# A recurrence's small products merged into fewer groups, with one place in PSUM per chunk

## The chip, the cores and the metric

The kernel runs on one core of one Trainium2 chip. The metric is the device time of one execution in microseconds, lower is better. The core has TensorE (matmul; its weight loads are a row of their own in the profile), VectorE, ScalarE, GpSimd (POOL) and SyncE (SP), each with a queue of its own that runs in program order, and DMA queues. Engines wait for each other by semaphores. Matmul results go to PSUM, in banks of 512 fp32 columns, and are read from there by VectorE or ScalarE.

## The reference, cut to what matters

One transformer block: a gated feed-forward part, a mixer, a cross attention to a memory, and a second feed-forward part. The mixer has two halves, side by side: eight heads of sparse attention and eight heads of a recurrence (RWKV-7). The change touches only the recurrence:

```python
def step(state, inp):
    r_t, w_t, k_t, v_t, kk_t, a_t = inp
    sa = jnp.einsum('bhvk,bhk->bhv', state, -kk_t)
    state = (state * w_t[:, :, None, :] + sa[..., None] * (kk_t * a_t)[:, :, None, :]
             + v_t[..., None] * k_t[:, :, None, :])
    return state, jnp.einsum('bhvk,bhk->bhv', state, r_t)
...
mu = jnp.mean(y, -1, keepdims=True)
var = jnp.mean(jnp.square(y - mu), -1, keepdims=True)
y = ((y - mu) * lax.rsqrt(var + RWKV_GN_EPS)).reshape(B, T, C)
```

## The kernel before

The sequence has 1,024 positions, and the recurrence is computed in 16 chunks of 64 (`NCH`, `CH`), each chunk for all eight heads, held as four pairs of 64 + 64 partitions (`PAIRS`). All its products are 64 rows by 64: those of a pair's first head use one corner of TensorE's array (rows and columns 0 to 63), those of the second the opposite one, so two run at a time. Eight products (four pairs by two heads) make one group; groups that write 128 columns are called wide.

Within a chunk, `gram_b`, `gram_k` and `gram_l` multiply the chunk's operands AR, B and K with each other; VectorE masks the results into GB, GK and L. `turn_a`, `turn_b` and `turn_k` turn (transpose) A, B and K by a product with the unit matrix `eye`. `x` multiplies GK by V. Then a triangular matrix is inverted by doubling, in five levels: `y0` to `y4` multiply the level's mask of GB (LTm, made by GpSimd) with T0; ScalarE copies the result to Y1; `t` and `tt` multiply it with the factor TT0, and VectorE adds the results to T0 and to TT0. T0 and TT0 are one matrix and its transpose, both carried along. `start` (lines 2081 and 2083) makes the first TT0 on VectorE. `wu`, `gr`, `s` and `out` make the state's step and the output, `mean` and `var` the normalisation: the mean comes from a product with `mean_pair`, VectorE subtracts it, ScalarE squares, a second product sums, VectorE inverts (`inverse`, line 2087).

Two chunks are under way at once. Each has its own tiles (`j` is the chunk's number modulo 2) and two banks of PSUM (`ps[j]`, used as `bank(j, 0)` and `bank(j, 1)`), and consecutive groups alternate between them.

The same stage, `attend_and_recur`, also does the attention half, on the same engines. One score step is `score` (TensorE, to `ar_s_ps`), `max` (VectorE: mask and smallest negative value, line 1999), `exp` (ScalarE) and `scale` (VectorE). `bank` transposes probabilities on TensorE, `copy` takes them to SBUF, `values` multiplies them by V, `finish` takes the result. The attention keeps one place for scores, so a score step waits for the `max` of the one before.

The order of all this is set by `joint_plan`. It is a list scheduler that runs when the program is built: every operation is an event with an engine, an assumed duration and the events that it needs, `in_order` replays them and picks on each engine the ready one of the longest remaining chain. It adds 0.1 us when TensorE's tiling changes (whole array, halves of columns for `values`, corners for the recurrence) and prefers to stay in one. Every engine then issues its events in that fixed order, whatever the real durations are. The masks and tables are loaded at the stage's start from ScalarE's queue, the values, keys and the next chunks' operands from SyncE's.

## Time and profile before

| what | value |
|---|---|
| time, median of 3 runs | 2672.34 us (2670.58 to 2675.16) |
| profiled execution, its own time | 2671.66 us |
| its span, first to last instruction | 2669.8 us |
| TensorE busy, share of the span | 97% |
| VectorE, ScalarE, GpSimd | 66%, 39%, 3% |
| the stage with the recurrence | 1083 to about 1665 us |

The span is that of one profiled execution; what lies around it (1.9 us) is launch and end. Busy time is the time in which at least one instruction of an engine runs; matmuls overlap each other, and their ends are modelled, so short stops of TensorE can hide in it. In a timeline row the first number is the start, the second the length; "idle before" is how long the engine stood, and the name behind the arrow is what it waited for. An fp32 product stands in the records twice, so a group of eight has 16 records. A name such as `ar_TT` is the tile TT0 of either chunk.

### The profile page before, as it was taken

Reading aid. Unit: us, or ns where it says so; the run is one execution under the profiler, and the core shown is the slowest. Engines: PE = TensorE matmul, PEld = TensorE weight load, DVE = VectorE, ACT = ScalarE, POOL = GpSimd, SP = SyncE. Lnnn points to the kernel's source line nnn. Section 1 sums busy time; section 2 is a strip of 40 time slices with the busy share of each in tenths; the row PEclk is TensorE's granted clock in tenths of the full one; section 3 lists DMA queues with packets and bytes.
Section 4 is the critical chain, followed back from the end, with each engine's and each line's share of the span. In section 5 each row is a group of like instructions: output and inputs, shape, how many; then the busy total and the mean of one; then the engine's idle time right before and its main releaser. Section 6 shows DMA issues by size and latency. Waiting matters only on the chain. (4 is left out here: it accounts for less than half of the span.)

```text
span 2669.8 us, 46706 instructions
## 1 busy us (share of the span) xinstructions
PE 2600.5 (97%) x19152; PEld 2151.7 (81%) x19152; DVE 1765.2 (66%) x2819; ACT 1041.2 (39%) x1839; POOL 88.0 (3%) x121
## 2 busy tenths in 40 slices
PE   8999999999999999899999998999999999999998
PEld 7788888888777788888888887777778788888887
DVE  6877667678344564577777775853446867667676
ACT  4332223445433534344444444542343332223443
POOL 0000000000000000111111110000000000000000
PEclk9999999999999999899999999999999999999999
DMA  4332335454423388521111110630022332335454
GB/s 143 111 105 76 118 114 180 151 196 155 99 95 102 104 265 219 138 50 36 34 38 38 30 42 6 248 135 1 32 102 80 110 116 70 113 114 192 139 190 145
DMA packets 268722, 295.65 MB, mean 111 GB/s; under 512 B 64898, under 2 KB 199296, under 8 KB 268544
## 3 DMA queue, kind: packets, MB, share of 16 engines
q1 hardware_dynamic: 265808, 290.47, 34.2%
q10 hardware_dynamic: 2736, 2.65, 0.4%
q8 instruction: 131, 2.15, 0.3%
q14 instruction: 47, 0.39, 0.0%
HBM read 206.47 MB, written 81.36 MB: 108 GB/s over the span
## 5 line engine op out<-in xcount | busy, mean ns | idle before, releaser
L1141 PE MATMUL f_ps<-hi,f_wh 128*128 128x512 f32 x672 | 263.1, 391 | 4.1 <-DVE f_wl L847 4.1
L1143 PE MATMUL f_ps<-hi,f_wl 128*128 128x512 f32 x672 | 262.9, 391 | 0.0
L2543 PE MATMUL f_ps<-hi,f_ahead_h 128*128 128x512 f32 x392 | 164.0, 418 | 0.8 <-PEq L72 0.8
L2544 PE MATMUL f_ps<-one_lo,f_ahead_h 128*128 128x512 f32 x392 | 153.6, 392 | 0.0
L2545 PE MATMUL f_ps<-hi,f_ahead_l 128*128 128x512 f32 x392 | 153.6, 392 | 0.0
L1141 PE MATMUL f_ps<-f_t3h,f_t2h 128*128 128x512 f32 x392 | 152.5, 389 | 0.0
L1142 PE MATMUL f_ps<-f_t3l,f_t2h 128*128 128x512 f32 x392 | 152.5, 389 | 0.0
L1143 PE MATMUL f_ps<-f_t3h,f_t2l 128*128 128x512 f32 x392 | 152.5, 389 | 0.0
L1141 PEld LDWEIGHTS f_ps<-hi,f_wh 128*128 128x128 f32 x672 | 127.0, 189 | 31.2 <-DVE f_wl L847 4.9
L1143 PEld LDWEIGHTS f_ps<-hi,f_wl 128*128 128x128 f32 x672 | 126.7, 189 | 26.4
L1142 PE MATMUL f_ps<-one_lo,f_wh 128*128 128x512 f32 x352 | 137.6, 391 | 0.0
L905 DVE TENSOR_TENSOR one_y<-f_ps,one_y 128x1024 f32<-128x1024 f32 x60 | 72.6, 1222 | 90.2 <-PE f_ps L1143 90.2
L905 DVE TENSOR_TENSOR y<-f_ps,y 128x1024 f32<-128x1024 f32 x60 | 72.6, 1222 | 90.2 <-PE f_ps L1143 90.2
L1142 PE MATMUL f_ps<-two_lo,f_wh 128*128 128x512 f32 x320 | 125.1, 391 | 0.0
L3270 PE MATMUL mt_d_ps<-mt_wh,hi 128*128 128x512 f32 x224 | 94.7, 423 | 10.1 <-DVE two_lo L3493 10.1
L2543 PEld LDWEIGHTS f_ps<-hi,f_ahead_h 128*128 128x128 f32 x392 | 74.0, 189 | 24.7 <-issue 10.4
L2544 PEld LDWEIGHTS f_ps<-one_lo,f_ahead_h 128*128 128x128 f32 x392 | 74.1, 189 | 18.5 <-issue 4.1
L3270 PE MATMUL mt_d_ps<-mt_wh,two_lo 128*128 128x512 f32 x224 | 88.2, 394 | 0.0
L3270 PE MATMUL mt_d_ps<-mt_wl,hi 128*128 128x512 f32 x224 | 88.2, 394 | 0.0
L2545 PEld LDWEIGHTS f_ps<-hi,f_ahead_l 128*128 128x128 f32 x392 | 74.0, 189 | 15.9
L1141 PEld LDWEIGHTS f_ps<-f_t3h,f_t2h 128*128 128x128 f32 x392 | 73.6, 188 | 15.4
L1143 PEld LDWEIGHTS f_ps<-f_t3h,f_t2l 128*128 128x128 f32 x392 | 73.6, 188 | 15.3
(584 smaller groups left out, 6830.4 us busy)
## 6 DMA issues: line engine op xcount, KB each, us to landing
act<-one_y SPq DMA_DIRECT2D x30, 512.0 KB, 3.5
f_work<-act SPq DMA_DIRECT2D x30, 512.0 KB, 3.6
act<-y SPq DMA_DIRECT2D x30, 512.0 KB, 3.6
arena<-act SPq DMA_DIRECT2D x30, 512.0 KB, 3.7
one_y<-in_w_in SPq DMA_DIRECT2D x25, 512.0 KB, 4.4
early<-in_ffn_w_gate SPq DMA_DIRECT2D x11, 1024.0 KB, 6.2
early<-in_ffn_w_up SPq DMA_DIRECT2D x11, 1024.0 KB, 8.7
f_raw<-in_ffn_w_gate SPq DMA_DIRECT2D x10, 1024.0 KB, 6.2
```

The costliest lines, as they stand in the source:

```text
L905: nc.vector.tensor_tensor(out, a, b, op).then_inc(joined, 1)
L1141: nc.tensor.matmul(out, wh, xh, start=start, stop=False)
L1142: nc.tensor.matmul(out, wh, xl, start=False, stop=False)
L1143: return nc.tensor.matmul(out, wl, xh, start=False, stop=stop)
L2543: nc.tensor.matmul(dense_ps[:, b, cols], w_hi[:, b, k, :], hi[:, k, cols], start=(k == 0), stop=False)
L2544: nc.tensor.matmul(dense_ps[:, b, cols], w_hi[:, b, k, :], lo[:, k, cols], start=False, stop=False)
L2545: mm = nc.tensor.matmul(dense_ps[:, b, cols], w_lo[:, b, k, :], hi[:, k, cols], start=False, stop=(k == KD - 1))
L3270: mm = nc.tensor.matmul(bank(n, b), lhsT[:, k, at], rhs[:, k, to], start=(k == 0 and x_ == 0), stop=(k == KD - 1 and x_ == 2))
```

## The change

It concerns the recurrence in `attend_and_recur`, its plan and one table. The operations, group by group:

- `gram_l` becomes a second part of `gram_b`: 16 products, one signal. VectorE reads it with two operations, GB and L, in a row.
- `turn_b` and `turn_k` become one group `turn_bk` of 16, `turn_a` and `x` one group `ax` of 16. ScalarE reads each with one copy of 512 columns for two of 256.
- In each level, `y` and a turning of T0 (a product with `eye`) are one group `yt` of 16, read by one copy of 512 columns into YT. The products `tt` and their adds on VectorE are gone for levels 0 to 3; in the last level `tf` makes the one result that is needed. `start` is gone.
- The mean is subtracted on TensorE, by a product with the table `center` (unit matrix less the mean). ScalarE copies the result to yT and squares it straight from PSUM.
- Each chunk has one place in PSUM, over both its banks: pairs 0 and 1 in the first, 2 and 3 in the second. Each group therefore waits until the group before it in its chunk has been read. `out` now waits for the reading of `s`.
- SyncE loads the next operands behind `ax` and no longer behind `turn_k`. `center` is one more load at the end of the tables.
- The plan has new assumed durations and needs; GpSimd's masking is due after `gram_b` rather than after `start`.

```diff
 FIRST_FILL = [FILLS.index((u, 0)) for u in range(UNITS)] + [len(FILLS)]
-PRODUCTS = ["gram_b", "gram_k", "gram_l", "turn_a", "turn_b", "turn_k", "x",
-            *[f"{w}{lv}" for lv in range(LEVELS) for w in (("y", "t", "tt") if lv + 1 < LEVELS else ("y", "tt"))],
-            "wu", "gr", "s", "out", "mean", "var"]
-TO_DVE = {"gram_b", "gram_k", "gram_l", "gr", "s", "mean", *[f"{w}{lv}" for lv in range(LEVELS) for w in ("t", "tt")]}
+PRODUCTS = ["gram_b", "gram_k", "turn_bk", "ax", *[f"{w}{lv}" for lv in range(LEVELS) for w in ("yt", "t") if (w, lv) != ("t", LEVELS - 1)],
+            "tf", "wu", "gr", "s", "out", "mean", "var"]
+TO_DVE = {"gram_b", "gram_k", "gr", "s", "tf", *[f"t{lv}" for lv in range(LEVELS - 1)]}
...
             before = {"gram_b": [out_of("var", c - 2)],
...
+                      "yt0": [out_of("ax"), ("masked", c)],
                       "s": [out_of("gr"), out_of("s", c - 1)],
-                      "out": [("rw", c, "s")],
-                      "mean": [out_of("out"), out_of("s")],
-                      "var": [("square", c)]}.get(name, [out_of(last)])
...
+                      "var": [("square", c)]}.get(name, [n and out_of(PRODUCTS[n - 1])])
...
-            if name == "gram_l":
-                event(("start", c), "dve", 0.6, out_of(name))
-                event(("masked", c), "pool", 4.6, ("start", c))
+            if name == "gram_b":
+                event(("masked", c), "pool", 4.6, out_of(name))
...
-        GB, GK, L = two("GB", 3, CH), two("GK", 2, CH), two("L", CH)
-        Ktok, AX = two("Kt", CH), two("AX", 2, CH)
+        GB, GK, L, AX = two("GB", 4, CH), two("GK", 2, CH), two("L", CH), two("AX", 2, CH)
...
-        T0, TT0, Y1 = two("T0", CH), two("TT0", CH), two("Y1", CH)
+        T0, YT = two("T0", CH), two("YT", 2, CH)
...
-                def at(k, p, h, width=CH):
-                    return ps[j][rows(h), k, p * width:(p + 1) * width]
+                def at(p, r, block, width=CH):
+                    return ps[j][rows(r), p // 2, (p % 2 * 4 + block) * CH:(p % 2 * 4 + block) * CH + width]
+
+                corners = [(p, r) for p in range(PAIRS) for r in range(2)]
+
+                def group(*parts):
+
+                    for block, lhsT_of, rhs_of, width in parts:
+                        for p, r in corners:
+                            mm = nc.tensor.matmul(at(p, r, block, width), lhsT_of(p)[rows(r)], rhs_of(p)[rows(r)], start=True, stop=True)
                     mm.then_inc(products[j], 1)
...
-                    group(0, B[j], AR[j], 2 * CH)
+                    group((0, lambda p: B[j][:, p], lambda p: flat(AR[j][:, p]), 2 * CH),
+                          (2, lambda p: AR[j][:, p][:, 0, :], lambda p: B[j][:, p], CH))
...
                     dve("gram_k")
+                    group((0, lambda p: B[j][:, p], unit, CH), (1, lambda p: K[j][:, p], unit, CH))
+                elif name == "ax":
+                    act("turn_bk")
                     pe.wait_ge(V_in[j], 32 * (c // 2 + 1))
-                    group(0, GK[j][:, :, 0, :], V[j])
...
+                    group((0, lambda p: AR[j][:, p, 0, :], unit, CH), (1, lambda p: GK[j][:, p, 0, :], lambda p: V[j][:, p], CH))
...
-                    group(0, LTm[j][:, lv], T0[j])
-                elif name[:2] == "tt":
-                    act(f"y{name[2:]}")
-                    group(0, Y1[j], TT0[j])
+                    group((0, lambda p: LTm[j][:, lv, p], lambda p: T0[j][:, p], CH), (1, lambda p: T0[j][:, p], unit, CH))
+                elif name == "tf":
+                    act(f"yt{LEVELS - 1}")
+                    group((0, lambda p: YT[j][:, p, 0, :], lambda p: YT[j][:, p, 1, :], CH))
                 elif name[0] == "t":
-                    act(f"y{name[1:]}")
-                    group(1, TT0[j], Y1[j])
+                    act(f"yt{name[1:]}")
+                    group((0, lambda p: YT[j][:, p, 1, :], lambda p: YT[j][:, p, 0, :], CH))
...
                 elif name == "out":
...
+                    pe.wait_ge(state, c + 1)
...
-                elif name[0] == "y":
-                    copy(Y1[j][:], bank(j, 0))
+                elif name[:2] == "yt":
+                    copy(both(YT[j][:]), result(j, 0, 2 * CH))
...
+                elif name == "mean":
+                    copy(yT[:, :, chunk(c)], features(j).rearrange("p (q c) -> p q c", c=CH))
...
-                    act.wait_ge(by_dve[j], through(dn, c, "mean"))
-                    nc.scalar.activation(ysq[j][:], yT[:, :, chunk(c)], ACT.Square).then_inc(by_act[j], 1)
+                    act.wait_ge(products[j], through(pn, c, "mean"))
+                    nc.scalar.activation(ysq[j][:].rearrange("p q c -> p (q c)"), features(j), ACT.Square).then_inc(by_act[j], 1)
...
+                    op(both(GB[j][:, :, 0:2, :]), result(j, 0, 2 * CH), gram_mask, ALU.mult)
+                    op(by_bank(L[j][:]), result(j, 2), all_pairs(m_low[:]), ALU.mult)
...
-                elif name[:2] == "tt":
-                    op(TT0[j][:], bank(j, 0), TT0[j][:], ALU.add)
+                elif name == "tf":
+                    op(by_bank(YT[j][:, :, 1, :]), result(j, 0), by_bank(YT[j][:, :, 1, :]), ALU.add)
...
-                    dve.wait_ge(by_act[j], through(an, c, "out"))
-                    op(yT[:, :, chunk(c)], yb[j][:], bank(j, 1), ALU.subtract)
...
-                elif e[0] == "start":
...
-                    nc.vector.tensor_tensor(TT0[j][:], GB[j][:, :, 0, :], over_pairs(m_one[:, 1]), ALU.mult).then_inc(by_dve[j], 1)
-                    dve.wait_ge(by_dve[j], through(dn, c, "one_t"))
-                    nc.vector.tensor_tensor(TT0[j][:], TT0[j][:], over_pairs(eye[:]), ALU.add).then_inc(by_dve[j], 1)
...
+        "center": np.eye(P, dtype=f) - same.astype(f) / f(CH),
```

Since the plan is computed anew, the events of attention stand elsewhere between those of the recurrence too. On TensorE, at the stage's opening, before (`ar_ps0` and `ar_ps1` are the places of chunk 0 and 1, `ar_s_ps` a score product):

```order
L1798 MATMUL ar_ps0<-chunk_ops 64x64 x8
L1798 MATMUL ar_ps1<-chunk_ops 64x64 x8
L1804 MATMUL ar_ps0<-ar_eye,chunk_ops 64x64 x8
L1804 MATMUL ar_ps1<-ar_eye,chunk_ops 64x64 x8
L1804 MATMUL ar_ps0<-ar_eye,chunk_ops 64x64 x8
L1804 MATMUL ar_ps1<-ar_eye,chunk_ops 64x64 x8
L1804 MATMUL ar_ps0<-ar_eye,chunk_ops 64x64 x8
L1804 MATMUL ar_ps1<-ar_eye,chunk_ops 64x64 x8
L1798 MATMUL ar_ps0<-ar_V0,ar_GK0 64x64 x8
L1798 MATMUL ar_ps1<-ar_V1,ar_GK1 64x64 x8
L1736 MATMUL ar_s_ps<-hi 128x128
L1737 MATMUL ar_s_ps<-hi 128x128
```

and now:

```order
L1797 MATMUL ar_ps0<-chunk_ops 64x128 x8
L1797 MATMUL ar_ps0<-chunk_ops 64x64 x8
L1797 MATMUL ar_ps1<-chunk_ops 64x128 x8
L1797 MATMUL ar_ps1<-chunk_ops 64x64 x8
L1735 MATMUL ar_s_ps<-hi 128x128
L1736 MATMUL ar_s_ps<-hi 128x128
L1797 MATMUL ar_ps0<-chunk_ops 64x128 x8
L1797 MATMUL ar_ps1<-chunk_ops 64x128 x8
L1735 MATMUL ar_s_ps<-hi 128x128
L1736 MATMUL ar_s_ps<-hi 128x128
L1797 MATMUL ar_ps0<-ar_eye,chunk_ops 64x64 x16
L1797 MATMUL ar_ps1<-ar_eye,chunk_ops 64x64 x16
```

The first rows before the first fence are four wide gram groups; what moved is that two score products now stand third and sixth, ahead of all the turning, where the first stood behind `x` of both chunks. On VectorE, which masks the gram results and reads the scores (lines 1999 and 1990 are `max`), the opening before:

```order
L2031 TENSOR_TENSOR ar_GK0<-ar_ps0,ar_m_gram 128x512
L2031 TENSOR_TENSOR ar_GK1<-ar_ps1,ar_m_gram 128x512
L2031 TENSOR_TENSOR ar_L0<-ar_ps0,ar_m_low 128x256
L2031 TENSOR_TENSOR ar_L1<-ar_ps1,ar_m_low 128x256
L2081 TENSOR_TENSOR ar_TT00<-ar_GB0,ar_m_one 128x256
L2083 TENSOR_TENSOR ar_TT00<-ar_TT00,ar_eye 128x256
L2081 TENSOR_TENSOR ar_TT01<-ar_GB1,ar_m_one 128x256
L2083 TENSOR_TENSOR ar_TT01<-ar_TT01,ar_eye 128x256
L1998 MEMSET ar_gate 128x1
L1999 ISA ar_sel,ar_bias<-ar_s_ps,ar_causal 128x128
L1999 ISA ar_bias 128x1
```

and now:

```order
L2022 TENSOR_TENSOR ar_L0<-ar_ps0,ar_m_low 128x256
L2022 TENSOR_TENSOR ar_GB1<-ar_ps1,ar_m_gram 128x4x128
L2022 TENSOR_TENSOR ar_L1<-ar_ps1,ar_m_low 128x256
L1989 MEMSET ar_gate 128x1
L1990 ISA ar_sel,ar_bias<-ar_s_ps,ar_causal 128x128
L1990 ISA ar_bias 128x1
L2022 TENSOR_TENSOR ar_GK0<-ar_ps0,ar_m_gram 128x512
L2003 RECIPROCAL ar_rden<-ar_den 128x1
L2005 TENSOR_TENSOR ar_coef<-ar_rden,gates 128x1
L2012 TENSOR_SCALAR ar_sel<-ar_sel,ar_coef 128x128
L2022 TENSOR_TENSOR ar_GK1<-ar_ps1,ar_m_gram 128x512
L1989 MEMSET ar_gate 128x1
```

The reading of GK for chunk 0 stood ahead of all attention and now stands behind the first `max`; for chunk 1 it stands behind the first `scale` as well; the four operations of `start` are gone. Further on, chunks 4 and 5 on VectorE (the stretch at 1217 us), before:

```order
L2031 TENSOR_TENSOR ar_L1<-ar_ps1,ar_m_low 128x256
L2012 RECIPROCAL ar_rden<-ar_den 128x1
L2014 TENSOR_TENSOR ar_coef<-ar_rden,gates 128x1
L2021 TENSOR_SCALAR ar_sel<-ar_sel,ar_coef 128x384
L2081 TENSOR_TENSOR ar_TT01<-ar_GB1,ar_m_one 128x256
L2083 TENSOR_TENSOR ar_TT01<-ar_TT01,ar_eye 128x256
L1998 MEMSET ar_gate 128x1
L1999 ISA ar_win,ar_bias<-ar_s_ps,ar_causal 128x384
L1999 ISA ar_bias 128x1
L2003 ISA ar_win,ar_bias<-ar_s_ps,ar_cmp_mask 128x63
```

and now:

```order
L2022 TENSOR_TENSOR ar_GB1<-ar_ps1,ar_m_gram 128x4x128
L2022 TENSOR_TENSOR ar_L1<-ar_ps1,ar_m_low 128x256
L1989 MEMSET ar_gate 128x1
L1990 ISA ar_sel,ar_bias<-ar_s_ps,ar_causal 128x384
L1990 ISA ar_bias 128x1
L1899 COPY ar_probT<-ar_t_ps 128x512
L2022 TENSOR_TENSOR ar_GK0<-ar_ps0,ar_m_gram 128x512
L2022 TENSOR_TENSOR ar_GK1<-ar_ps1,ar_m_gram 128x512
L1989 MEMSET ar_gate 128x1
L1990 ISA ar_win,ar_bias<-ar_s_ps,ar_causal 128x384
```

The two operations on `ar_TT01` that stood ahead of the window's `max` are gone; the readings of GK0 and GK1 stand there now.

## Rows read from the trace of the kernel before

**Rows 1.** The page, busy time by engine.

```profile
PE 2600.5 (97%) x19152; PEld 2151.7 (81%) x19152; DVE 1765.2 (66%) x2819; ACT 1041.2 (39%) x1839; POOL 88.0 (3%) x121
```

**Rows 2.** Windows: length, busy us (records) by engine, granted clock, DMA share, GB/s.

```profile
1083.00:1099.00 16.00, 10.76 (x232) 9.88 (x232) 7.35 (x17) 4.98 (x13) 9.80 (x16) 0.98 0.98 278
1099.00:1112.00 13.00, 12.66 (x160) 11.31 (x161) 8.33 (x44) 3.71 (x17) 1.51 (x3) 0.50 0.08 18
1112.00:1140.00 28.00, 28.00 (x595) 25.16 (x594) 19.63 (x111) 12.89 (x51) 0.00 (x0) 1.00 0.17 47
...
1157.00:1160.00 3.00, 0.95 (x14) 0.81 (x10) 2.33 (x6) 0.73 (x3) 2.91 (x5) 0.97 0.07 13
1160.00:1164.00 4.00, 4.00 (x46) 3.10 (x45) 3.07 (x14) 1.17 (x5) 0.00 (x0) 0.59 0.01 4
...
1293.00:1297.00 4.00, 2.03 (x24) 1.25 (x22) 3.27 (x11) 1.52 (x5) 0.99 (x2) 0.92 0.00 0
1297.00:1300.00 3.00, 3.00 (x32) 2.32 (x28) 1.93 (x9) 1.35 (x4) 0.00 (x0) 0.53 0.20 46
...
1640.00:1665.00 25.00, 21.38 (x362) 17.25 (x358) 9.31 (x15) 6.94 (x17) 0.00 (x0) 1.00 0.01 2
1083.00:1665.00 582.00, 563.37 (x9840) 479.45 (x9840) 426.48 (x1360) 256.55 (x745) 87.23 (x116) 0.98 0.16 40
```

**Rows 3.** Timeline, 1218 to 1221 us: start, length, engine, what [idle before].

```profile
1218.39 0.94 DVE L2081 TENSOR_TENSOR ar_TT<-ar_GB,ar_m_one 128x256 f32<-128x256 f32 x1
...
1219.37 0.83 DVE L2083 TENSOR_TENSOR ar_TT<-ar_TT,ar_eye 128x256 f32<-128x256 f32 x1
...
1220.89 0.45 PE L1736 MATMUL ar_s_ps<-hi 128*128 128x384 f32 x1 [1.03 <-DVE ar_bias L2003]
```

**Rows 4.** Timeline of TensorE, inside a group of s.

```profile
1645.07 0.28 PE L1868 MATMUL ar_ps<-ar_V,ar_Kt 64*64 64x64 f32 x4
...
1645.42 0.28 PE L1868 MATMUL ar_ps<-ar_V,ar_Kt 64*64 64x64 f32 x4
```

**Rows 5.** Timeline of TensorE, groups behind each other.

```profile
1299.95 0.68 PE L1798 MATMUL ar_ps<-ar_V,ar_GK 64*64 64x64 f32 x16
1300.46 0.63 PE L1798 MATMUL ar_ps<-ar_Y,ar_TT 64*64 64x64 f32 x16
1301.03 0.66 PE L1764 MATMUL ar_o_ps<-ar_probT,ar_vw 128*64 128x128 f32 x8
```

**Rows 6.** Groups by shape in the stage: count | busy us, mean ns | idle before.

```profile
L2031 DVE TENSOR_TENSOR ar_TT<-ar_ps,ar_TT 128x256 f32<-128x256 f32 x80 | 33.5, 421 | 19.3 <-PE ar_ps L1798 18.7
...
L1947 ACT COPY ar_Y<-ar_ps 128x256 f32<-128x256 f32 x80 | 29.6, 371 | 68.0 <-PE ar_ps L1798 67.8
...
L2083 DVE TENSOR_TENSOR ar_TT<-ar_TT,ar_eye 128x256 f32<-128x256 f32 x16 | 13.4, 837 | 0.6
...
L2031 DVE TENSOR_TENSOR ar_GB<-ar_ps,ar_m_gram 128x512 f32<-128x512 f32 x16 | 10.7, 676 | 9.4 <-DMA ar_m_gram<-in_m_gram 9.2 <-PE ar_ps L1798 0.2
...
L2081 DVE TENSOR_TENSOR ar_TT<-ar_GB,ar_m_one 128x256 f32<-128x256 f32 x16 | 10.3, 646 | 0.0
...
L1947 ACT COPY ar_WU<-ar_ps 128x512 f32<-128x512 f32 x16 | 9.3, 582 | 12.1 <-PE ar_ps L1798 12.1
```

**Rows 7.** The opening: DMA issues with KB and us to landing, then timeline rows.

```profile
ar_kc<-kc_lo SPq DMA_DIRECT2D x1, 31.5 KB, 4.8
...
ar_row_ok<-in_mask_row_ok ACTq DMA_DIRECT2D x1, 0.5 KB, 6.5
...
1086.22 0.60 SPq L1664 DMA_DIRECT2D ar_kc<-kc_lo  x1
...
1087.61 0.52 ACTq L1970 DMA_DIRECT2D ar_row_ok<-in_mask_row_ok  x1
...
1096.22 0.33 PE L1798 MATMUL ar_ps<-ar_V,ar_GK 64*64 64x64 f32 x4 [3.06 <-issue]
```

**Rows 8.** Waits in the stage: us in total, times, longest.

```profile
PEld ar_ps L1798 <- DVE ar_TT L2031: 0.7, 2, 0.5
```

More of the change, by code:

```diff
@@ L1472, in joint_plan @@
-            if name[:2] == "tt":
-                before = [("rw", c, last), out_of(f"y{lv}")]
-            event(("rw", c, name), "pe", 0.92 if name in WIDE else 1.35 if name in ("s", "out") else 0.47, *before)
-            after = {"gram_k": [out_of("gram_b")], "gram_l": [out_of("gram_k")], "turn_b": [out_of("turn_a")],
-                     "turn_k": [out_of("turn_b")], "x": [out_of("turn_k")],
-                     "s": [c and ("rw", c - 1, "out")]}.get(name, [])
-            if name[:2] == "tt" and f"t{lv}" in PRODUCTS:
-                after = [out_of(f"t{lv}")]
@@ L1627, in attend_and_recur @@
         pn = numbered(PRODUCTS)
-        dn = numbered(["gram_b", "gram_k", "gram_l", "one_t", "start", *[x for x in PRODUCTS if x in TO_DVE and x[0] == "t"], "gr_r", "gr", "mean"])
-        an = numbered(["turn_a", "turn_b", "turn_k", "x", *[f"y{lv}" for lv in range(LEVELS)], "wu", "out", "square", "var"])
+        dn = numbered(["gram_b", "gram_l", "gram_k", *[f"t{lv}" for lv in range(LEVELS - 1)], "tf", "gr_r", "gr"])
+        an = numbered(["turn_bk", "ax", *[f"yt{lv}" for lv in range(LEVELS)], "wu", "out", "mean", "square", "var"])
         gn = numbered(["one", "start", *[f"lev{lv}" for lv in range(LEVELS)]])
@@ L1855, in recur @@
                 elif name == "gr":
                     act("wu")
-                    group(0, WU[j][:, :, 0, :], GB[j][:, :, 1:3, :], 2 * CH)
+                    group((0, lambda p: WU[j][:, p, 0, :], lambda p: flat(GB[j][:, p, 1:3, :]), 2 * CH))
                 elif name == "s":
                     dve("gr")
-                    for p in range(PAIRS):
-                        if p == 0 and c:
-                            pe.wait_ge(state, c)
-                        if p == 0 and not c:
-                            pe.wait_ge(zeroed, 1)
-                        terms = ((Ktok[j][:, p], V[j][:, p]), (GB[j][:, p, 2, :], WU[j][:, p, 1, :]), (GR[j][:, p, 1, :], M[j][:, p]))
-                        for n, (lhsT, rhs) in enumerate(terms):
-                            for h in range(2):
-                                mm = nc.tensor.matmul(at(1, p, h), lhsT[rows(h)], rhs[rows(h)], start=(n == 0), stop=(n == 2))
@@ L1869, in recur @@
-                    mm.then_inc(products[j], 1)
-                elif name == "out":
-                    for p in range(PAIRS):
-                        terms = ((V[j][:, p], GK[j][:, p, 1, :]), (WU[j][:, p, 1, :], GB[j][:, p, 1, :]), (M[j][:, p], GR[j][:, p, 0, :]))
-                        for n, (lhsT, rhs) in enumerate(terms):
-                            for h in range(2):
-                                mm = nc.tensor.matmul(at(0, p, h), lhsT[rows(h)], rhs[rows(h)], start=(n == 0), stop=(n == 2))
-                    mm.then_inc(products[j], 1)
+                    if c:
+                        pe.wait_ge(state, c)
+                    else:
+                        pe.wait_ge(zeroed, 1)
@@ L3615, in first_keys @@
                     c, which = n // 4, n % 4
[L3616 to L3617 removed]
+                    load_op(sp, c, which, ops, ops_dram, ops_in)
                 elif kind == "keys":
```

174 lines of the change are left out of this document (79 added, 95 removed).

## The prediction, made before the run

> **What bounds the kernel now.** I read the page's busy line first: TensorE is busy 97% of the span and VectorE 66% [rows 1]. The change lies in one stage, from 1083 to about 1665 us, so the next view is the table of windows over it. TensorE is busy for 563.4 of its 582 us [rows 2], VectorE for 426 and ScalarE for 257. The reader should see that TensorE's work is the floor and that there is little else to win: 18.6 us of idle, in three places. The opening (1083 to 1112) has 5.2 + 0.3, the tail (1640 to 1665) has 3.6, and the other 9.5 us are scattered, two of them as single gaps of 2.05 and 1.97 us at 1157 and 1293 [rows 2]. There is a second loss in the same table. After the idle opening the granted clock is 0.50 for 13 us, and after either single gap it is 0.59 and 0.53. At the rate of 1112 to 1140 (595 matmuls in 28 us, 21 per us), 160 matmuls are worth 7.5 us where 13 were spent: 5.5 lost. By the same rate the 46 matmuls of 1160 to 1164 lose 1.8 us and the 32 of 1297 to 1300 lose 1.5, together some 3 us.
>
> What TensorE waits for, where it waits, is read in the timeline around 1220 us: two VectorE operations of `start`, 0.94 and 0.83 us, stand ahead of the operation that reads the scores, and the next score product waits 1.03 us for it [rows 3]. VectorE isn't the bound on average, but where the recurrence's small operations bunch ahead of a `max`, it holds up TensorE.
>
> **TensorE's work.** A chunk's recurrence had 234 products on TensorE in 27 groups (three of 8 gram, three of 8 turned, 8 for x, 5 of 8 for y, 4 of 8 for t, 5 of 8 for tt, wu, gr, 24 for s, 24 for out, mean, var). It now has 242 in 20 groups: the 40 products of tt become 40 turnings of T0, and `tf` adds 8. In the s group three terms (six products) start 0.35 us after each other [rows 4], so a 64-column product costs 58 ns, and 16 x 8 more of them cost 128 x 0.058 = **+7.4 us**. (The Trainium skill, TensorEngine Tiling (Array Packing), section Instruction Overhead, gives about 60 cycles for each matmul whatever its size. At 2.4 GHz the sum would have 128 x 0.025 = 3.2 us here; the spacing in the trace is over twice that, each product standing in it as two records, and the trace's number is used.)
>
> Against that stand the ends of groups. Eight products take 8 x 58 = 0.47 us, and from one corner group's start to the next corner group's pass 0.51 us, to the start of a group of another tiling 0.57 [rows 5]: an end costs 0.05 us, leaving the corners 0.10. In TensorE's order, counted over the stage, a corner group is followed by another 222 times before and 146 times now, by something else 178 times before and 142 now. That is 76 x 0.05 + 36 x 0.10 = 7.4 us at most. Not every end costs its 0.05 (gram groups in a row show less), so I take 6.0. **Work: +7.4 - 6.0 = +1.4 us**, with bounds 0 and +3.8 (if only the tiling counts).
>
> **VectorE and ScalarE.** VectorE loses `start` (0.65 + 0.84 us), four of five adds net (4 x 0.42; five tt go, `tf` comes) and the subtraction of the mean (of the adds' shape, taken at 0.42 too) [rows 6]: 3.6 us a chunk, 57 us of its 426. ScalarE's five copies grow from 256 to 512 columns, 0.37 to 0.58 us; four small ones become two wide ones (4 x 0.37 to 2 x 0.58), and a copy for the mean is new: 5 x 0.21 - 0.32 + 0.37 = +1.1 us a chunk, 18 us on an engine busy 257 of 582 [rows 2, 6]. I cost that at nothing: the work of attention on TensorE covers it. Uncovered, it would be 0.21 us at each of 80 levels, 17 us.
>
> A level's own chain is near even: y 0.47, copy 0.37, t and tt 0.94, adds 0.42 behind (2.2) against yt 0.93, copy 0.58, t 0.47, add 0.42 (2.4). The single place in PSUM makes gram_k wait for gram_b's and L's reading, turn_bk for gram_k's, ax for turn_bk's; before, every second one could go ahead. In the new order at least one step of another chunk or of attention stands between any two groups of a chunk, and more than one in all but 23 cases, so most of a hop of about 1.4 us (0.68 for GB, 0.42 for L, of the adds' shape, and the signals; [rows 6]) is covered.
>
> **The waits in the middle.** 9.5 us of idle and 3 us of slow clock. The gap at 1220 has its cause removed. Those at 1157 and 1293 come behind a pile on VectorE of which `start` is a part, but `inverse` and `scale` the other, and those remain. With 13% less on VectorE (57 of 426) and no 1.5 us block ahead of scores I take three quarters of the idle, -7.5 us (bounds -3 and -9.5), and the clock with it, -3 (bounds 0 and -3). Waits of 0.2 to 0.3 us, hidden in the modelled ends of matmuls, should thin out with 112 fewer groups: -1.5.
>
> **The opening, where the change costs.** The first score product now stands third on TensorE, behind both gram_b, and waits for the keys' last load: issued at 1086.22, landing 4.8 us later, at 1091.0 [rows 7]. The two gram_b last 2 x (0.87 + 0.47) = 2.7 us, until 1085.8, so TensorE stands 5.3 us. On VectorE max_0 now stands ahead of the reading of gram_k, and waits for the masks: row_ok, issued at 1087.61, lands 6.5 us later, at 1094.1. Score 1 waits for max_0, 1.3 us; turn_bk of both chunks is queued behind it, and the second GK also behind scale_0, which needs exp_0: some 0.9 together, an estimate from GK's 0.68 us, of GB's shape, behind max_0 [rows 6] and as much behind scale_0, less the 0.35 us or so of score work between. Sum 7.5, against 5.5 now, of which 3.06 was a stop with no releaser in the trace (issue) [rows 7] that the new waits would cover. **+2.0 us**. The clock at half for 13 us I leave as it is (bounds -5 and +4 for a shorter or longer stretch). The tail's order is near the same: 0.
>
> **Sum.** +1.4 - 7.5 - 3.0 - 1.5 + 2.0 = -8.6 us. The profiled execution took 2671.66 us (its span 2669.8), so 2663.1; the median of the runs, 2672.34, is 0.7 above it: **2663 us**, by 0.35% faster.
>
> **Rivals.**
> *Waits only move (2667 to 2677).* The PE order was laid out by the plan with other takes, and new joints wait: if only a third of the middle's idle goes (-3), no clock, and the opening costs 4 more, the sum is +1.4 - 3 - 0 - 1.5 + 6 = +3. For it: VectorE's pile consists mostly of attention's operations. Against: the one gap that can be traced in full comes from `start` [rows 3].
> *More comes out (2648 to 2655).* Idle and dips in the middle go wholly and the opening's stretch at half clock shortens: +1.4 - 9.5 - 3 - 1.5 + 2 - 5 = -15.6, some 2656 to 2650. For it: both chunks now start their levels at once rather than one after the other.
> *Slower, by serial reading of PSUM (over 2678).* One mechanism: with one place in PSUM a group can't be written until its last result is read out, so each joint of a chunk whose cover is thinner than the hop stops TensorE. 20 joints in each of 16 chunks are 320. The forecast turns to +5.3 us from an uncovered 14/320 = 0.044 us a joint, or from 0.22 us at the 64 joints of gram, turn and ax alone; at 0.1 us a joint it is +32 - 8.6, 2695. For it: in 23 places a single step is all the cover. Against: TensorE hardly waits for the recurrence's results now, with 103 places of a single step; the row of its waits for tt's adds reads 0.7 us in the whole stage [rows 8]. (The Trainium skill warns in TensorEngine Tiling (Array Packing), section PSUM Bottleneck, that tiling speeds up the products but not their evacuation, which may become the bottleneck. By that rule ScalarE's 18 us more would come out at the end; ScalarE's 44% busy speaks against it.)
> *It does not do what it says.* The products aren't fewer, 242 for 234; if group ends cost nothing and VectorE's relief opens nothing, +7.4 + 2 = +9. It belongs to the slower case.
>
> **Chances.** Forecast as reasoned (2655 to 2667) 0.54; more 0.16; waits move 0.21; slower 0.09. A measurement of this kernel tells 0.2%, 5.3 us, from no change: faster 0.70, same 0.21, slower 0.09. The range goes from 2652, leaving some 0.08 of the large gain out, to 2673, leaving the upper half of "waits move" and the slower case, 0.12.
>
> **What would show it.** In the new profile: 10,096 matmul records in the stage, 256 more than now; a stage of about 573 us; VectorE's busy time in it down by some 57 us and ScalarE's up by 18; first score product at 1091 with a wait on a load of 5 us; TensorE's idle in the middle below 3 us and no stretch at half clock there. Wrong would be: TensorE waiting for copies of the recurrence (yt, ax, turn_bk) in many places; reading across two banks slower than 0.68 or 0.58 us for 512 columns; a second long stretch at half clock at the start.

## The result, and the profile after

The changed kernel takes **2654.57 us** (median of 4 runs, 2653.67 to 2658.34), the kernel before took 2673.47 on the same chip (4 runs, 2670.58 to 2675.16). The ratio is **0.9934, 95% interval 0.9922 to 0.9946**: 18.9 us or 0.7% faster. A second measurement, of five executions, gave 0.9950 (0.9937 to 0.9964), 2655.93 us against 2670.45. The forecast was 2663, 9.3 us below the kernel before, with a range of 2652 to 2673. The sign and the range held, but the gain is 1.5 to 2 times the one forecast, and both measurements lie in the lower quarter of the range.

The profiled execution of the changed kernel took 2655.38 us, its span 2653.6. Its busy line, which answers to [rows 1]:

```profile
PE 2592.8 (98%) x19408; PEld 2149.1 (81%) x19408; DVE 1718.3 (65%) x2707; ACT 1058.7 (40%) x1823; POOL 82.0 (3%) x121
```

TensorE has 256 records more than before and is busy 8 us less. VectorE has lost 47 us, ScalarE has gained 17.5. Where the time went is in the windows, to be held against [rows 2] (length, busy us and records by engine, granted clock, DMA share, GB/s). The stage now begins at 1082.35 and ends at 1649.83:

```profile
1082.00:1099.00 17.00, 10.82 (x197) 10.11 (x197) 5.76 (x18) 3.30 (x7) 10.55 (x18) 0.80 0.77 238
1099.00:1112.00 13.00, 13.00 (x324) 11.97 (x324) 6.82 (x42) 7.60 (x24) 0.00 (x0) 1.00 0.29 65
...
1112.00:1625.00 513.00, 510.56 (x9210) 437.26 (x9204) 357.76 (x1174) 256.13 (x682) 70.77 (x98) 1.00 0.14 36
1625.00:1650.00 25.00, 22.44 (x380) 18.18 (x376) 8.97 (x13) 7.00 (x19) 0.00 (x0) 1.00 0.01 2
1082.00:1650.00 568.00, 556.82 (x10096) 477.52 (x10096) 379.31 (x1247) 274.03 (x729) 81.32 (x116) 0.99 0.16 42
```

Three things are to be seen. In the long middle TensorE stands 513.00 - 510.56 = 2.4 us, where it stood 9.4 in 528 before (528.00 less 518.57, the row below), and its clock is 1.00. The 13 us behind the opening hold 324 matmuls at a clock of 1.00, where [rows 2] had 160 at 0.50. And the stage is 567.5 us long, 13.6 less than the 581.0 of before (1083.08 to 1664.12).

The same stretch in the kernel before, which [rows 2] has only in part:

```profile
1112.00:1640.00 528.00, 518.57 (x9096) 441.01 (x9095) 401.48 (x1285) 240.92 (x701) 75.93 (x98) 0.99 0.14 35
```

The opening itself, TensorE's timeline (start, length, what, [idle before]):

```profile
1082.35 2.90 PE L1797 MATMUL ar_ps<-chunk_ops 64*64 64x128 f32 x64 [1.78 <-PEq L72]
1091.08 0.44 PE L1735 MATMUL ar_s_ps<-hi 128*128 128x128 f32 x1 [5.84 <-DMA ar_kc<-kc_lo]
...
1091.66 3.68 PE L1797 MATMUL ar_ps<-chunk_ops 64*64 64x128 f32 x32
1095.28 0.47 PE L1735 MATMUL ar_s_ps<-hi 128*128 128x128 f32 x1
```

Score 0 starts at 1091.08, behind 5.84 us of standing for the keys' last load, as foretold. Its product takes 0.44 us where the next score products at full clock take 0.33, and gram_k's 32 records take 3.68 us: this is the half clock. The clock's own records in the traces have it at half from 1089.36 on for 6.83 us (before: from 1098.40 on, 13.65 us), so that its first 1.7 us fall into the wait. A "stretch at half clock" below is always such a record.

And the groups that read the recurrence's results, to be held against [rows 6] (count | busy us, mean ns | idle before):

```profile
L2022 DVE TENSOR_TENSOR ar_T<-ar_ps,ar_T 128x256 f32<-128x256 f32 x64 | 26.8, 422 | 16.4 <-PE ar_ps L1797 15.6
...
L2022 DVE TENSOR_TENSOR ar_GB<-ar_ps,ar_m_gram 128x512 f32<-128x512 f32 x16 | 10.8, 677 | 11.6 <-DMA ar_m_low<-in_m_low 9.7 <-PE ar_ps L1797 1.9
```

```profile
L1939 ACT COPY ar_YT<-ar_ps 128x512 f32<-128x512 f32 x80 | 46.3, 582 | 35.2 <-PE ar_ps L1797 34.9
```

A reading that lies over two banks costs what one within a bank did: 677 ns for 676, 582 for 582, 422 for 421.

### The profile page after: what moved, and what is told of

Its sections match the earlier page's. It is cut to its first block and busy times, and to the rows that moved or that the text cites. A ratio compares the mean times of both kernels' runs of the same rounds, so it can differ in the third digit from the quotient of the medians.

```text
span 2653.6 us, 47043 instructions
## 1 busy us (share of the span) xinstructions
PE 2592.8 (98%) x19408; PEld 2149.1 (81%) x19408; DVE 1718.3 (65%) x2707; ACT 1058.7 (40%) x1823; POOL 82.0 (3%) x121
## 5 line engine op out<-in xcount | busy, mean ns | idle before, releaser
L1142 PEld LDWEIGHTS f_ps<-f_t3l,f_t2h 128*128 128x128 f32 x392 | 73.6, 188 | 15.3
```

The costliest lines, as they stand in the source:

```text
L1142: nc.tensor.matmul(out, wh, xl, start=False, stop=False)
```

## The experiments

The prediction had a theory, **A**: VectorE held up TensorE where its small operations bunched, less work on it takes those waits away, and the new products on TensorE cost nearly what the fewer groups give back. Its rival was that the waits only move. The runs add one that it did not have: that the gain is the new plan's (it has other assumed durations, and so another order on every engine). Every ratio below is to runs of the kernel before on the same chip. The length of the stage is the finer measure: ahead of it, where no edit reaches, the profiled executions took between 1078.8 and 1084.0 us.

**1. The changed kernel again**, for the comparisons of the first four.

> The changed kernel itself, so that the others of this call have it beside them on one chip. Both theories: 2652 to 2658 us, a ratio to the kernel before of 0.992 to 0.995.

Measured: 2655.93 us, ratio 0.9950 (0.9937 to 0.9964); stage 567.4 us, the same stretch of 6.83 us at half clock.

**2. The kernel before with less on VectorE.**

```diff
-                    op(TT0[j][:], bank(j, 0), TT0[j][:], ALU.add)
+                    op(TT0[j][:, 0, 0:1], bank(j, 0)[:, 0, 0:1], eye[:, 0:1], ALU.add)
...
+                    all_ = slice(None) if c < 2 else slice(0, 1)
-                    nc.vector.tensor_tensor(TT0[j][:], GB[j][:, :, 0, :], over_pairs(m_one[:, 1]), ALU.mult)...
+                    nc.vector.tensor_tensor(TT0[j][:, all_], GB[j][:, all_, 0, :], over_pairs(m_one[:, 1])[:, all_], ALU.mult)...
```

> The kernel before, in its own order, but VectorE leaves nearly all of the second factor out: the two operations of start (from chunk 2 on) and all five adds of tt touch one column instead of 256, so the inversion is wrong; TensorE does every product as before, each signal stays. VectorE has some 45 us less. Theory A (most of the stage's gain is TensorE's waits for VectorE going, and the half-clock stretches behind them): the idle of the middle, 9.5 us, falls below 3, the stretches at 1160 and 1297 go, and the time is 8 to 13 us below the kernel before, 2660 to 2665. Theory B (the gain is in fewer groups and their ends on TensorE, and in the order): at most 3 us below, 2670 to 2674.

Measured: 2661.89 us, ratio 0.9967 (0.9955 to 0.9978), 8.6 us less than before. Stage 575.1 us, 6.0 less. What was left out was less than the text above says: the adds have one column, but `start` keeps one pair, 64 columns, and its two operations still take most of their time (the last section says beside what they run):

```profile
L2084 DVE TENSOR_TENSOR ar_TT<-ar_TT,ar_eye 128x64 f32<-128x64 f32 x14 | 9.3, 662 | 0.5
L2082 DVE TENSOR_TENSOR ar_TT<-ar_GB,ar_m_one 128x64 f32<-128x64 f32 x14 | 5.7, 404 | 0.0
```

TensorE in the middle (the window of before, 1112 to 1640):

```profile
1112.00:1640.00 528.00, 522.78 (x9240) 445.37 (x9235) 378.73 (x1278) 240.90 (x695) 70.93 (x98) 1.00 0.14 35
```

5.2 us of idle for 9.4, not the "below 3" of theory A, and of the two stretches at half clock the first is still there (3.41 us at 1155.03). With nothing changed but 23 us of VectorE's work gone (401.48 to 378.73 in this window), about half of the gain is there. The time lies where theory A had it, the waits went by half only. And one thing isn't separated here: `start` now lasts 1.07 us for the 0.6 of the plan, where it lasted 1.48, so the plan has become truer too.

**3. The changed kernel with VectorE's work put back**: six operations of 128x256 a chunk into a tile that nobody reads, two behind the reading of gram_b and one behind each of four t.

```diff
+                more(over_pairs(m_gram[:, 0]), over_pairs(m_one[:]), ALU.mult)
+                more(over_pairs(m_gram[:, 1]), over_pairs(eye[:]), ALU.add)
...
+                more(over_pairs(m_low[:]), over_pairs(eye[:]), ALU.add)
```

> The changed kernel with VectorE's work put back, on a tile that nobody reads: two operations of 128x256 from SBUF behind each L, one behind each add to T0, in all 6 a chunk and some 45 us; nothing waits for them but VectorE's own next operations. Theory A: TensorE waits for scores again, 5 to 12 us above the changed kernel, 2660 to 2667. Theory B: within 2 us of it.

Measured: 2665.66 us, ratio 0.9982 (0.9973 to 0.9991), 9.7 us over the changed kernel; stage 577.3 us, the idle in the middle is back at 8.2, with one stretch of 3.41 us at half clock in it. VectorE got back 35 us of the 47 (1753.2 busy for 1718.3):

```profile
1112.00:1640.00 528.00, 519.78 (x9322) 443.75 (x9318) 390.81 (x1273) 257.95 (x686) 74.23 (x98) 1.00 0.14 35
```

The plan doesn't know of these operations, as the plan of before didn't know how long `start` is. So this run shows what unplanned work on VectorE costs; number 11 puts work back that is planned.

**4. The changed kernel with each yt group cut in two**, 80 more groups with the same products; 48 of their ends lie between corner groups, 32 before something else.

```diff
-                    group((0, lambda p: LTm[j][:, lv, p], lambda p: T0[j][:, p], CH), (1, lambda p: T0[j][:, p], unit, CH))
+                elif name[:2] == "ya":
+                    group((0, lambda p: LTm[j][:, lv, p], lambda p: T0[j][:, p], CH))
...
+                    group((1, lambda p: T0[j][:, p], unit, CH))
```

> The changed kernel with each level's yt issued as two groups of 8, each with its own signal and its own place in the plan (80 groups more, the same products, one read). In TensorE's order 48 more corner groups follow a corner group and 32 more leave the corners. With the prediction's prices, 48 x 0.05 + 32 x 0.10 = 5.6 us above the changed kernel, 2658 to 2662, which is theory A's. Theory B needs much more for 80 ends, since the change took away 112: 12 us or over, 2667 or more. If ends cost nothing, 0 to 1.

Measured: 2663.41 us, ratio 0.9975 (0.9966 to 0.9984), 7.5 us over the changed kernel, the stage 6.9 us longer (574.4). Idle in the middle is hardly a part of it (528.00 less 525.14 busy, 2.9 us for 2.4), and the opening's stretch at half clock is the same, 6.83 us. So 48 ends at 0.05 and 32 at 0.10 us, 5.6 together, cost 6.9 to 7.5, some 20 to 35% more, and fewer and larger groups give what the prediction counted for them or a little more.

**5. The changed kernel with each turning twice**, 640 products more and nothing else.

```diff
-                    group((0, ...T0[j][:, p], CH), (1, lambda p: T0[j][:, p], unit, CH))
+                    group((0, ...T0[j][:, p], CH), (1, lambda p: T0[j][:, p], unit, CH), (1, lambda p: T0[j][:, p], unit, CH))
```

> The changed kernel with each turning of T0 issued twice into the same place: 8 more products in each of 80 levels, 640 in all, and no group, copy or wait more. It prices the product on the corners. If a product costs what the s group's spacing says, 58 ns, and TensorE's work is the floor: +37 us on the changed kernel. If most of a product lies in the time that TensorE would stand for copies anyway (the levels bound by their hops): under +20 us. If a product costs what a serial reading of 60 cycles at 2.4 GHz would say (Trainium skill, TensorEngine Tiling (Array Packing), section Instruction Overhead): +16 us. The work on TensorE was sized with it, so the +7.4 us of the prediction stands or falls by this run.

Measured: 2694.69 us, ratio 1.0087 (1.0072 to 1.0101). The changed kernel's ratio was 0.9934 and 0.9950, so the 640 products cost 1.4 to 1.5% of 2672, 37 to 41 us; the stage went from 567.5 to 605.6 us, 38.1 us, **59.6 ns a product** for the 58 of the prediction. Its opening has 10.24 us at half clock for 6.83; without the 0.7 us or so that this costs (an estimate: half of the busy time in either stretch) it is 58.6. They aren't hidden in any wait: TensorE's work is the floor. (The Trainium skill, TensorEngine Tiling (Array Packing), section Instruction Overhead, puts some 60 cycles of overhead on each matmul. At 2.4 GHz that would be an estimated 16 us for the 640; by this run an fp32 product on these corners costs over twice that.)

**6. The kernel before, planned anew**: its plan is told that `start` takes 1.5 us.

```diff
-                event(("start", c), "dve", 0.6, out_of(name))
+                event(("start", c), "dve", 1.5, out_of(name))
```

> The kernel before, its plan told that start takes 1.5 us on VectorE and not 0.6 (which the trace shows); nothing else. The order of steps on all engines is laid out anew, the work is the same. It separates new durations in the plan from less work on VectorE. Theory A (less work on VectorE is what took the waits away): within 2 us of the kernel before. Rival P (the new plan's better durations are the gain): 4 to 9 us faster than before, and TensorE's idle in the middle down from 9.4 us to under 6.

Measured: **2658.48 us, ratio 0.9941 (0.9928 to 0.9953)**, 13.7 us less than before. This is the surprise of the study, and it goes against theory A as the only cause: the work of the kernel before, in another order, is as fast as the changed kernel within what the measurements tell. The stage is 568.5 us long, 1.0 more than in the changed kernel. The windows:

```profile
1100.00:1113.00 13.00, 11.26 (x150) 9.89 (x152) 8.82 (x51) 5.89 (x24) 2.63 (x4) 0.61 0.03 7
...
1113.00:1628.00 515.00, 514.10 (x9108) 438.74 (x9106) 396.70 (x1281) 241.55 (x698) 73.92 (x98) 1.00 0.14 36
```

TensorE's idle in the middle is 0.9 us, with all of VectorE's work in place. The opening is as it was, 150 matmuls in 13 us at a clock of 0.61 and 13.65 us at half clock in all, so it is the middle alone that has gained.

**7. The changed kernel with an error of the same size in its plan**: the reading of gram_b and L declared 0.9 us too short, as `start` was.

```diff
-OUT_OF = {"gram_b": 1.1, ...
+OUT_OF = {"gram_b": 0.2, ...
```

> The changed kernel, its plan told that the reading of gram_b and L takes 0.2 us on VectorE and not 1.1, so that it errs by 0.9 us a chunk at the same place as the plan of the kernel before did with start (0.6 for 1.5). Nothing else is changed. Since telling the plan of before the right duration won as much as the whole change, the question is whether the changed kernel needs its right durations. Theory P (the plan's durations carry the gain, and less work on VectorE nothing): 8 to 14 us slower than the changed one, TensorE's idle in the middle back at 7 us or more. Theory R (either remedy is enough: VectorE has room again, or the plan knows that it has none): at most 4 us slower, idle in the middle under 4.

Measured: 2654.68 us, ratio 0.9933 (0.9920 to 0.9947), what the changed kernel has. Its profiled execution happens to be the slowest of its five (2660.35), so its rows aren't those of the median: idle in the middle is 4.8 us, and the opening has 17 us at half clock (3.41 and 13.65):

```profile
1098.00:1111.00 13.00, 13.00 (x173) 12.04 (x170) 5.38 (x35) 5.49 (x20) 0.00 (x0) 0.50 0.14 32
```

```profile
1111.00:1628.00 517.00, 512.23 (x9241) 438.51 (x9240) 359.19 (x1169) 254.90 (x675) 70.45 (x98) 1.00 0.14 36
```

By the times theory R holds. By that trace's idle it is between the two (theory R said under 4, theory P 7 or more): twice the idle of the changed kernel.

**8. Both at once on the kernel before**: the edits of 2 and 6.

> The kernel before with both at once: the plan told 1.5 us for start, and start's two operations (from chunk 2 on) and all five tt adds touching one column, so that this part of the computation is left out. Alone the first won 13.7 us and the second 8.6. Theory R (both take away the same waits): within 3 us of the replanned kernel alone, some 2656 us. If the work on VectorE costs time of its own: the gains add, 6 to 9 us faster than the replanned kernel, some 2650 us.

Measured: 2654.23 us, ratio 0.9933 (0.9919 to 0.9946); the replanned kernel alone had 0.9941 (0.9928 to 0.9953). That is 0.8 parts in a thousand, 2 us, where 8.6 came before planning, and theory R by the letter. But the intervals are over 3 us wide to either side, and the stage is 564.4 us, 4.1 less than in number 6, so the times alone don't decide between 2 us and 6. The middle does:

```profile
1112.00:1622.00 510.00, 509.97 (x9022) 435.40 (x9024) 370.27 (x1265) 239.66 (x690) 68.78 (x98) 1.00 0.14 36
```

No idle is left, and there was only 0.9 us for the second remedy to take away. The other 3 us of the stage lie in its opening, where TensorE stands 5.1 us for 6.9 and is at half clock for 10.24 us for 13.65.

TensorE's idle in the middle of the stage, in all kernels that bear on the two theories:

| plan | VectorE's work | idle, us |
|---|---|---|
| before, `start` at 0.6 | all | 9.4 |
| before, `start` at 0.6 | less (2) | 5.2 |
| before, `start` at 1.5 | all (6) | 0.9 |
| before, `start` at 1.5 | less (8) | 0.0 |
| changed | as changed | 2.4 |
| changed, told 0.9 too little (7) | as changed | 4.8 |
| changed | 35 us more, unplanned (3) | 8.2 |
| changed, `start` planned (11) | 12 us more, planned | 0.8 |

Less work takes about half of the idle away, the new order nearly all of it.

**9. The changed kernel with score 0 behind chunk 1's ax**, as the kernel before has it.

```diff
-        event(("score", s), "pe", 0.113 * n + 0.1 + extra, s and ("max", s - 1))
+        event(("score", s), "pe", 0.113 * n + 0.1 + extra, s and ("max", s - 1) or ("rw", 1, "ax"))
```

> The changed kernel, its plan told that the first score product comes behind chunk 1's ax, so that TensorE opens with both gram_b, gram_k, turn_bk and ax and score 0 behind them, as in the kernel before. It tests the opening, which the prediction put 2 us dearer and which came out 2.4 us cheaper. Theory O (the prediction's): the order of the opening costs, TensorE stands 5 us for the keys ahead of work that it could do. Then this kernel is 2 to 5 us faster than the changed one, the wait for the keys is gone and the stretch at half clock is about as long as in the changed one (6.8 us) or longer by less than the gain. Theory H: the order of the opening is what shortened the stretch at half clock, since the standing takes the slow time into itself. Then TensorE works through its first products sooner, but a stretch of 10 to 14 us at half clock lies over score work, and the kernel is 1 to 4 us slower than the changed one. Rest of the stage the same in both.

Measured: 2656.11 us, ratio 0.9941 (0.9926 to 0.9956); stage 567.5 us, the same as with the changed kernel to 0.1. Both theories missed. (The account further below puts the opening at 3.9 us cheaper than before, not at the 2.4 of this text.) The wait for the keys is gone and others are in its place (3.1 us for the reading of L, 2.4 for which the trace has no releaser), and the half clock comes in two stretches of 3.41 us, not in one of 10 to 14:

```profile
1080.00:1096.00 16.00, 10.29 (x227) 9.98 (x229) 3.33 (x6) 1.76 (x3) 10.56 (x18) 0.89 0.91 277
1096.00:1110.00 14.00, 13.94 (x326) 12.91 (x321) 7.87 (x44) 8.40 (x22) 0.00 (x0) 0.88 0.16 36
```

**10. The changed kernel with the keys loaded first**, ahead of V, and the score masks ahead of `eye` and the level masks.

```diff
-            for c in range(2):
-                load_v(c)
...
+            for c in range(2):
+                load_v(c)
```

> The changed kernel with the keys' loads ahead of V's on SyncE's queue, and the score masks ahead of eye and the level masks on ScalarE's. It takes away the cause of the opening's wait (keys landing at 1091). If the wait for the keys costs what it lasts, score 0 starts at about 1088.6 and the kernel is 2 to 4 us faster than the changed one. If what waits next (V for ax, eye for turn_bk, the masks for the reading of the scores) or a longer stretch at half clock takes it back: within 1 us, or slower.

Measured: 2654.08 us, ratio 0.9933 (0.9920 to 0.9946); stage 567.5 us. The wait for the keys shrank from 5.84 to 2.03 us, and nothing came of it:

```profile
1084.20 0.30 PE L1735 MATMUL ar_s_ps<-hi 128*128 128x128 f32 x1 [2.03 <-DMA ar_kc<-kc_lo]
...
1088.95 0.33 PE L1735 MATMUL ar_s_ps<-hi 128*128 128x128 f32 x1 [1.94 <-DVE ar_bias L1993]
```

Score 1 stands for the reading of score 0 now, and more short waits follow. In the first 30 us of the stage TensorE stands 5.5 us in number 9 and 6.1 in number 10, for the 5.8 of the changed kernel. That fits an opening bound by how soon the first operands, masks and readings are there at all, and not by which of them TensorE takes first; no run shows it directly.

**11. start back on VectorE, planned at its true length.** If a well-planned VectorE has room, then the first level needn't turn T0 on TensorE.

```diff
-                    group((0, ...T0[j][:, p], CH), (1, lambda p: T0[j][:, p], unit, CH))
+                    group((0, ...T0[j][:, p], CH), *([(1, lambda p: T0[j][:, p], unit, CH)] if lv else []))
...
+            if name == "gram_k":
+                event(("start", c), "dve", 1.5, out_of(name))
...
+                    nc.vector.tensor_tensor(YT[j][:, :, 1, :], GB[j][:, :, 0, :], over_pairs(m_one[:, 1]), ALU.mult)...
+                    nc.vector.tensor_tensor(YT[j][:, :, 1, :], YT[j][:, :, 1, :], over_pairs(eye[:]), ALU.add)...
```

> The changed kernel with the first turned T0 made by VectorE again (the two operations of start, planned at 1.5 us, read from GB), so that TensorE's first level has 8 products and not 16 and ScalarE's first copy 256 columns and not 512. TensorE loses 16 x 8 products, VectorE gets 16 x 1.5 = 24 us. If TensorE's work is the floor and VectorE's work costs nothing once it is planned right: 128 x 0.058 = 7.4 us faster than the changed kernel, 2647 to 2649 us. If VectorE's operations hold up the reading of scores again: within 2 us of it or slower.

Measured: 2651.50 us (2646.20 to 2653.88), ratio 0.9923 (0.9909 to 0.9936). The median lies above the 2647 to 2649 forecast, and by the ratios the gain on the changed kernel is 3 to 7 us. The stage of the profiled execution, its fastest, is 561.6 us, 5.9 less than the changed kernel's for the 7.4 forecast, with 128 products less and VectorE's 12 us more (not 24) beside them. VectorE doesn't hold up TensorE again; idle is 0.8 us in the middle:

```profile
1109.00:1616.00 507.00, 506.21 (x9038) 432.02 (x9036) 367.60 (x1196) 251.61 (x680) 71.13 (x98) 1.00 0.15 37
```

**12. The edits of 10 and 11 together.**

> The kernel with start on VectorE and the changed kernel's merged products, with the keys' loads ahead of V's and the score masks ahead of eye and the level masks on the queues. The work in the stage is that of the former, 6 to 8 us less on TensorE than in the changed kernel. If the opening gives something once the load orders are changed (with the changed kernel alone they gave some 1 us at most): 2648 to 2650. If the waits of the opening are taken over by the next wait: 2650 to 2653, as without them. As a version that should be ahead of both kernels: faster than before by 0.8 to 0.95%, than the changed kernel by 2 to 6 us.

Measured: **2646.83 us (2646.20 to 2650.34), ratio 0.9913 (0.9900 to 0.9927)**; stage 559.8 us. It is the fastest version, a little below both forecasts: 0.9% under the kernel before, and some 0.2 to 0.4% under the changed kernel by the ratios of both. Whether the order of the loads has a part in that is open: the stage is 1.7 us shorter than in number 11, but it gave nothing on the changed kernel, and the intervals of 11 and 12 overlap.

## Why the prediction held, and which steps failed

The stage lost 13.6 us where 8.6 were forecast; another 2.7 lie outside it (0.7 ahead of it, 2.0 behind), where the change does nothing. Point by point, by the prediction's own sum:

- **Work and hidden waits, +1.4 - 1.5 = -0.1**: seen +0.9, what remains of the 13.6 when the rows below are taken off. The product's price is confirmed by itself (59.6 ns for 58), the group ends a little too low (6.9 to 7.5 us for 5.6 in number 4). How the small remainder divides between work and waits that no row shows is not settled, and no run shows the -1.5 for hidden waits by itself.
- **Idle in the middle, -7.5**: seen 9.4 - 2.4, -7.0. **The clock there, -3**: no stretch at half clock is left, -3.3 by the prediction's reading of [rows 2] (1.8 and 1.5). Both sizes were right, and in part by luck, for the reason given for them was half of the truth. The prediction put it all on less work on VectorE. Number 2 shows this cause at work, but with the old plan it took half of the idle, and number 6 takes 8.5 of the 9.4 us away by order alone. A new order came with the change, and the prediction mentions the plan only as a risk ("with other takes", in the rival that waits only move), not as a cause of gain. Number 8 shows that the two remedies remove the same waits; number 7 that with the work gone a wrong duration costs nothing clear in time, though idle doubled in its trace; numbers 3 and 11 that work which the plan doesn't know of brings the waits back, and planned work doesn't. What stands against TensorE is VectorE's work that the order isn't laid out for. What share of the changed kernel's gain belongs to less work and what to the new order can't be said, since they don't add.
- **The opening, +2.0**: the step that failed; seen -3.9. Of its terms the first was right to 0.1 us in time (score 0 at 1091.08, standing 5.84 for the 5.3 forecast), so the idle is 5.8 us for 5.6. The 1.3 us for score 1 and the 0.9 behind it don't appear: gram_k, 3.68 us long at half clock, covers them. The large term is the clock, which was "left as it is": 13.65 us at half became 6.83, a quarter of that inside the wait. By the rate of 1112 to 1140 the 197 matmuls of 1082 to 1099 are worth 9.4 of the 10.82 us busy, so 1.4 are lost where 5.5 were. The bound of -5 covered it, the chosen value did not. It was also in the rival "more comes out", which had a chance of 0.16, and in whose 2648 to 2655 the first median lies (the second is just above). That rival's own sum, -15.6, gives 2656 to 2657, though, just outside its range.
- **The tail, 0**: -0.3 (idle 2.7 before its end, 2.4 now).
- **Outside the stage, nothing forecast**: the part behind it is 2.0 us shorter. The kernel before had a stretch of 3.41 us at half clock at 2091.68 there, the changed one none in either of its profiled executions; in numbers 9, 10 and 12 it is there again with the changed kernel's work behind the stage, and in number 2 it is absent with that of before. So it doesn't go with the change.
- **ScalarE's 18 us, costed at nothing**: 17.5 us more (256.55 to 274.03), and TensorE waits for a copy of yt, ax or turn_bk in no row of the changed kernel's waits. **VectorE's 57 us** came to 47. By the groups it is 57: start's 23.7, four adds of five net 26.7, the mean's 6.7 us are gone. But an operation's duration reaches into the next one (in the timeline of number 6 two adds of 0.42 us start 0.34 apart, 0.08 us), and busy time counts that once: for 112 instructions less, 9 us, an estimate from that one spacing. The prediction subtracted sums of durations from a busy time.
- **The rival of serial reading** fell: readings over two banks keep their prices, and the longest wait of TensorE for a reading of the recurrence in the middle is this (0.2 us in total, one time, 0.2 the longest):

```profile
PE ar_ps L1797 <- DVE ar_L L2022: 0.2, 1, 0.2
```

Why the opening's time at half clock is shorter stays open. In one profiled execution each it was 10 to 14 us in all four kernels with the structure of before, 17 in number 7, and 3.4 to 10.2 us in all others of the changed structure. Number 9 speaks against the place of score 0 as the cause: the time is the same 6.83 us, in two parts. The one thing that goes with it is the order of the loads: both kernels with the keys first (10 and 12) have 3.41 us where the same kernels without it have 6.83. Two pairs don't show a cause, and in number 10 the stage gained nothing by it.

And one doubt on number 6: it is a single new order. That the duration is now true is one reason why it should be better; that the old order was simply an unlucky one among many isn't excluded. No run gave the plan a false duration that reshuffles as much on the kernel before.

## What to carry to other kernels

When a change also feeds new numbers to a planner, run the old kernel with the corrected numbers first: here the order that came of one corrected duration (1.5 for 0.6 us) was worth as much as the whole restructuring. Two remedies for the same waits don't add, so once the order is right, move work off the engine that is the floor, even onto the one that seemed to be in the way: that is what numbers 11 and 12 did. And the time at half clock behind an idle opening was worth some 4 us here; it belongs in the range, and a guess at it does not decide a forecast.

## What the runs showed of the hardware that was not expected

VectorE's scalings, products and adds between tiles of SBUF last longer while GpSimd works. The timeline of number 6, with GpSimd's masks from 1212.04 for 2.89 us, and the same two operations right behind:

```profile
1212.04 2.89 POOL L1697 TENSOR_TENSOR ar_LTm<-ar_GB,ar_m_lev 128x256 f32<-128x256 f32 x4
...
1212.82 0.85 DVE L2021 TENSOR_SCALAR ar_win<-ar_win,ar_coef 128x384 f32<-128x384 f32 x1
...
1213.58 0.71 DVE L2024 TENSOR_SCALAR ar_win<-ar_win,ar_coef 128x63 f32<-128x63 f32 x1
...
1215.09 0.42 DVE L2021 TENSOR_SCALAR ar_win<-ar_win,ar_coef 128x384 f32<-128x384 f32 x1
...
1215.42 0.25 DVE L2024 TENSOR_SCALAR ar_win<-ar_win,ar_coef 128x63 f32<-128x63 f32 x1
```

0.85 for 0.42 us at 384 columns, 0.71 for 0.25 at 63: what is added to a scaling is 0.43 to 0.46 us, whatever its width (at 896 columns 1.12 for 0.69 in the trace of before). `start` with a quarter of its columns still took 0.40 and 0.66 (number 2) for 0.65 and 0.84. Number 11 shows best that GpSimd is the cause: there 9 of the 16 `start` are clear of its masks, and their second operation takes 0.42 us, where the 7 beside them take 0.83. Operations that read PSUM keep their price in the same stretch (a reading of scores at 384 columns takes 0.55 us either way), and so do the reciprocals of one or two columns (0.15). The Trainium skill, SBUF — State Buffer, section Who interferes with whom, says that VectorE and GpSimd share a pair of ports under an exclusive lock, held for a whole instruction, and that VectorE meets it with two inputs in SBUF, or in the two-port modes that copies and scalings can enter. The rows agree with an operation that waits out part of a GpSimd one (0.72 us each here), and with PSUM as one of two inputs keeping clear of it; they don't show the lock.

The delay seems to go both ways: with VectorE's operations made narrow or left out and the order the same, GpSimd's own busy time fell from 85.9 us (number 6) to 80.8 (number 8) and from 88.0 (before) to 83.0 (number 2), at the same 121 instructions. What an operation between tiles of SBUF costs therefore depends on where the order puts it, and that is a second thing besides the queue that a planner with fixed durations doesn't see.
